# Reordering ScalarE's SSD distances and VectorE's decayed x in a one-core diffusion-backbone step

## What is computed

```
a_cs   = cumsum(dt * a)                                      # one row of 128 per head
lmat   = exp(a_cs[l] - a_cs[s]) where s is not later than l, else 0
y_diag = sum_s (C[l].B[s]) * lmat[l,s] * dt[s] * x[s]
states = sum_s B[s] * exp(a_cs[last] - a_cs[s]) * dt[s] * x[s]
y_off  = C[l] . states_in * exp(a_cs[l])
y      = (y_diag + y_off, both directions, + x * d_skip) * silu(z)
y      = rmsnorm over the 512 channels of the group
```

## Time and profile before

| What | Value |
|---|---|
| Median of three runs | 1797.37 us (1796.99 to 1802.09) |
| The profiled execution's own time | 1797.12 us |
| Its span (first to last recorded work) | 1795.3 us |
| TensorE busy | 1560.0 us (87%) |
| VectorE, ScalarE, GpSimd busy | 479.0, 324.8, 88.8 us |
| Mean granted TensorE clock | 0.976 of full |
| Units of the SSD stage | about 136 to 412 us of the span |

### The profile page before, as it was taken

One profiled execution on the slowest core, in us unless ns is written; L12 is line 12 of the kernel. 1 busy time (PEld: TensorE's weight loads), 2 busy tenths in 40 slices (PEclk: granted clock), 3 DMA queues, 4 the chain that ended last, 5 costly groups with the idle time before them and its releaser, 6 DMA issues.

```text
span 1795.3 us, 22496 instructions
## 1 busy us (share of the span) xinstructions
PE 1560.0 (87%) x9269; PEld 925.9 (52%) x9269; DVE 479.0 (27%) x1189; ACT 324.8 (18%) x893; POOL 88.8 (5%) x116
## 2 busy tenths in 40 slices
PE   6997988999999999998999888777878777977776
PEld 4654445455545555555666545444455444544443
DVE  2336666761003555524211110000010000100003
ACT  1336445440001222111110100000000000000001
POOL 0002122110000000100000000000000000000000
PEclk9998999999999999998999999999989999999999
DMA  8234333312431433465799999999999999999995
GB/s 342 94 108 164 106 106 124 134 59 94 187 117 59 188 141 123 168 261 200 318 428 426 429 427 427 427 427 429 426 417 427 427 427 428 427 427 427 428 427 227
DMA packets 40449, 512.91 MB, mean 286 GB/s; under 512 B 4624, under 2 KB 4752, under 8 KB 10528
## 3 DMA queue, kind: packets, MB, share of 16 engines
q1 hardware_dynamic: 34272, 489.89, 65.9%
q0 software_dynamic: 5936, 21.01, 3.5%
q10 hardware_dynamic: 144, 0.59, 0.1%
HBM read 506.65 MB, written 4.82 MB: 285 GB/s over the span
## 4 chain that ended last, share of the span: by engine, by line
PE 52%; DMA 31%; DVE 8%; ACT 6%; issue 2%; SPq 0%; DVEq 0%; ACTq 0%; POOL 0%
DMA arena<-in_expert_chunks 31%; PE psum L975 17%; PE psum L651 7%; PE psum L407 5%; PE psum L623 5%; PE psum L418 4%; ACT arena L1265 3%; PE psum L815 2%; PE psum L707 2%; PE psum L430 1%; ACT arena L1277 1%; PE psum L699 1%; PE psum L458 1%; DVE arena L1668 1%; PE psum L923 1%
## 5 line engine op out<-in xcount | busy, mean ns | idle before, releaser
L975 PE MATMUL psum<-arena 128*64 128x256 f32 x6144 | 708.7, 386 | 138.0 <-DMA arena<-in_expert_chunks 105.4
L975 PEld LDWEIGHTS psum<-arena 128*64 128x64 f32 x6144 | 442.0, 138 | 398.1 <-DMA arena<-in_expert_chunks 149.5
L2075 DVE TENSOR_TENSOR arena<-arena,psum 128x256 f32<-128x256 f32 x64 | 26.9, 421 | 704.8 <-ACT arena L1426 704.8
L407 PE MATMUL psum<-arena 128*128 128x384 f32 x512 | 168.9, 487 | 2.8 <-ACT arena L1184 2.8
L407 PEld LDWEIGHTS psum<-arena 128*128 128x128 f32 x512 | 96.2, 190 | 68.6 <-issue 3.3
L651 PE MATMUL psum<-arena 128*128 128x384 f32 x384 | 129.4, 491 | 0.0
L418 PE MATMUL psum<-arena 128*128 128x512 f32 x288 | 128.0, 600 | 0.0
L1426 ACT ACTIVATE arena<-psum 128x256 f32<-128x256 f32 x64 | 24.6, 384 | 563.4 <-PE psum L975 563.4
L1434 ACT ACTIVATE arena<-psum 32x256 f32<-32x256 f32 x126 | 47.3, 375 | 276.4 <-PE psum L975 275.3
L651 PEld LDWEIGHTS psum<-arena 128*128 128x128 f32 x384 | 72.5, 193 | 46.9 <-issue 3.0
L418 PEld LDWEIGHTS psum<-arena 128*128 128x128 f32 x288 | 55.8, 195 | 69.3 <-issue 68.5
(11 more groups left out here) (273 smaller groups left out, 1137.1 us busy)
## 6 DMA issues: line engine op xcount, KB each, us to landing
arena<-in_expert_chunks SPq DMA_DIRECT2D x191, 2048.0 KB, 25.4
arena<-in_mixer_chunks SPq DMA_DIRECT2D x40, 2048.0 KB, 8.3
arena<-cs_rows POOLq DMA_DIRECT2D x24, 512.0 KB, 4.9
arena<-in_h_cm POOLq DMA_DIRECT2D x8, 256.0 KB, 3.1
out_state<-arena POOLq DMA_DIRECT2D x8, 256.0 KB, 2.5
arena<-in_x_cm SPq DMA_DIRECT2D x1, 1536.0 KB, 8.6
arena<-in_expert_chunks SPq DMA_DIRECT2D x1, 1536.0 KB, 31.7
arena<-in_x_sample POOLq DMA_DIRECT2D x1, 1024.0 KB, 6.7
```

The source lines that it names most:

```text
L407: mm = pe.matmul(b[:, 0:NTOK], w[:, k, ct * P:(ct + 1) * P], src[:, k, :], start=k == 0, stop=k == KT - 1)
L975: mm = pe.matmul(psum[HALF * q:HALF * (q + 1), bank, 0:2 * P], src[:, k0 + k, :], w_k[:, 2 * P * q:2 * P * (q + 1)], start=bool(opens and ...
```

## The change

ScalarE makes `distances(1)` before the loop, and in unit u it makes `distances(u+2)` between the side items and the wait for `y_ready`, where it made `distances(u+1)` ahead of `decays(u+1)`. VectorE makes the chunk-0 `decayed` of both directions right after the three copies of x, and the other two behind the state copies of the same unit t = 0, so that t = 1 has none (and loses its wait for `x_ready`); `mean_square(u-1)` now comes behind `farther(u+1)` and ahead of `masked(u+1)`. No instruction is added or taken away.

```diff
             items([("z", 0, 2)])
+            distances(1)
             for u, (g, t) in enumerate(units):
                 if u + 1 < len(units):
-                    distances(u + 1)
                     decays(u + 1)
                 items(beside(g, t))
+                if u + 2 < len(units):
+                    distances(u + 2)
                 act.wait_ge(sem("y_ready"), u + 1)
@@
             for u, (g, t) in enumerate(units):
                 hd = slice(S_HPG * g, S_HPG * (g + 1))
-                if u:
-                    mean_square(u - 1)
                 if t == 0:
                     for tt in range(NT):
                         b = x_take()
                         x_free(dve.tensor_copy(xTM[:, tt, :], b[:, :]))
                     x_settle()
+                    decayed(0, 0, g)
+                    decayed(1, 0, g)
                 if u + 1 < len(units):
                     farther(u + 1)
+                if u:
+                    mean_square(u - 1)
+                if u + 1 < len(units):
                     masked(u + 1)
-                if t < 2:
-                    if t == 1:
-                        dve.wait_ge(sem("x_ready"), n_x[0])
-                    decayed(0, t, g)
-                    decayed(1, 2 * t, g)
                 if u:
                     rstd_of(u - 1)
@@
                         x_free(dve.tensor_copy(st_out[:, d, :], b[:, :]))
+                    decayed(0, 1, g)
+                    decayed(1, 2, g)
                 if t == 1:
```

## The result

The changed kernel takes 1769.86 us, the median of four runs (1766.51 to 1772.40), beside 1799.73 us for the kernel before in the runs it was compared with (four, 1796.99 to 1804.40). The ratio is 0.983 with a 95% interval of 0.9816 to 0.9844, some 30 us faster; the forecast was 1765 us. The profiled execution takes 1766.51 us with a span of 1764.7, 30.6 us less than the 1795.3 of before.

A forecast was written before the change was run, and what follows sets the result against it. The ScalarE-VectorE loop of square, distances and farther bounds the SSD stage, TensorE following. Gains 7.5 (group 0) + 21.6 (groups 1, 2) + 3.8 (group 3) = 32.9 us off 1797.12: 1764.2, given as 1765 us; eight in ten 1759 to 1777.

The forecast's parts named there:

- Rival B: Behind the SSD stage: the microseconds saved do not reach the end, total within 5 us of before; chance 0.03.
- t = 0, group 0: First unit of the stage: no square before it, so it only loses 1.2 us for the two decayed behind the state copies.
- t = 1, group 0: ScalarE's gap there is 2.68 us, so the distances come 2.1 us late and 3.3 us is gained.
- t = 2, group 0: Farther starts at y ready, with square, distances and handover no longer ahead of it: gain 5.4 us.
- t = 0, groups 1 and 2: Farther starts 2.3 us sooner, two decayed behind the state copies cost 1.2 us: net gain 1.1 us each.
- t = 1, groups 1 and 2: Farther starts at most 1.1 us late, as the distances overfill ScalarE's 3.71 us gap: gain 4.3 us each.
- t = 2, groups 1 and 2: Farther starts at y ready itself, the square beside it and the mean behind: gain 5.4 us each.
- group 3: TensorE binds there; its first state matmul starts at 4.0 us after y ready, not waiting for decayed x: gain 3.8 us.
- C: ScalarE stands at the late distances in all units, the farther waits 5.4 us as before: about 1801 us; chance 0.01.
- D: ScalarE's distances wait for their cumulative sums, rows landing over 15 us later, holding up the square: 1846 us; chance 0.02.
- rival A: TensorE takes over in groups 0 to 2, with 1.2 GHz spells after waits: gain 21 us, 1776 us; chance 0.13.
- loss bound: VectorE's two decayed at the t = 0 product's start: one decayed lost, 0.6 us a group, 2.4 us over four groups.

The follow-up runs named there:

- e1: Kernel before with only ScalarE's part of the change (distances made earlier), VectorE's order as before: 1770.41 us, ratio 0.9841 to the kernel before.
- e2: Changed kernel with ScalarE's loop of before, so only VectorE's part of the change: 1800.65 us, ratio 1.001 to the kernel before.
- e4: Changed kernel with distances of u+2 made before the first tanh in t = 0 and t = 1 of groups 0 to 2: 1762.75 us.
- e5: Changed kernel with both the second two decayed moved ahead of the weights and the distances made before the first tanh: 1758.68 us, ratio 0.9777.
- e6: Changed kernel with GpSimd's product cut to one head of eight, the other heads' weights in the chunk left at zero: 1753.52 us, ratio 0.9744.
- e7: Changed kernel with the mean of the square put back ahead of the copies and the farther: 1772.31 us, ratio 0.9851 to the kernel before.
- e3: Changed kernel with the second two decayed moved from behind the state copies to ahead of the weights of t = 0: 1764.54 us, ratio 0.9808.

## Why the prediction was right

**What bounds.** Right, and shown by e1 and e2: with the loop shortened the time goes although a part of TensorE's waits stays; with the waits for the decayed x removed and the loop left, they come back elsewhere and the time stays.

**That nothing is lost behind the stage.** Right. The span from L623's first matmul on is 1383.6 us before and 1383.2 after, and between 1382.0 and 1385.0 in all ten traces. Rival B falls.

**The sum.** Predicted 32.9 us for the profiled execution, 30.6 came. The stage itself gave 31.6; 1.5 us went ahead of it, where the change does nothing (below). Unit by unit:

| Term | predicted gain | measured |
|---|---|---|
| t = 0, group 0 | -1.2 | -1.0 |
| t = 1, group 0 | 3.3 | 4.1 |
| t = 2, group 0 | 5.4 | 4.5 |
| t = 0, groups 1 and 2 | 1.1 each | 1.7, 1.3 |
| t = 1, groups 1 and 2 | 4.3 each | 4.4, 4.4 |
| t = 2, groups 1 and 2 | 5.4 each | 4.5, 4.5 |
| group 3 | 3.8 | 3.3 |

That the sum came so near is in part luck. In group 0, 7.6 us for 7.5, two errors cancel: t = 2 gave 0.9 less and t = 1 gave 0.8 more. Unit 1 of the kernel before was 0.7 us longer than unit 4, because ScalarE stood 1.44 us at 183.16 for the z tile behind TensorE's wait of 7.76 us, where unit 4 has 0.52; in the changed kernel neither wait is there. The prediction, which let TensorE follow everywhere, had no term for it. The t = 0 units gave more than 1.1 us; between their own 1.7 and 1.3 stands the instruction held up by GpSimd's product, 3.08 us before in unit 3 and 2.72 in unit 6, 2.7 after in both.

**The distances' room.** Predicted 1.0 to 1.1 us late, 1.03 measured, and e4 got back 1.1, 1.1 and 2.1 us. Rivals C and D fall: in groups 1 and 2 no farther but those of t = 1 waits for the distances, and the distances at 245.98 us follow the tanh at 245.44 with no wait for their rows.

**The terms that were mis-sized.** First t = 2, 4.5 us instead of 5.4. The step counted VectorE and ScalarE and let TensorE follow. But TensorE waits 2.5 to 5.1 us at L605 in t = 1 and comes out of it with the clock granted in part at its 1.2 GHz level (0.50 of full over the four L605 matmuls in unit 1, 0.77 in unit 4), and the tile behind takes 8.18 us. So the second z tile is late: ScalarE stands 1.20 us for it in unit 5 and 2.19 in unit 2. This is rival A, come true in small, 0.9 us a group and not 4. That two so different delays cost the same has a reason in the rows: with either, VectorE's first L1561 comes beside GpSimd's product and ends 0.5 us behind it (262.54 us after a product that ends at 261.99 in unit 5; 200.33 after 199.79 in unit 2), and the second tanh and the second L1561 still follow. In e4, where the wait at L605 was 1.61 us, the slow tile was absent, the first of the two ran ahead of the product, and unit 5 took 16.14 us, the 16.3 that was predicted. In e5 it is unit 2 that takes 16.13 us, with a tile of 7.03 us behind a wait of 2.09, and unit 5 that takes 17.18, with a tile of 8.02 us behind one of 2.14. In e6, where the product is small, lateness costs its size: unit 2 stands 0.48 us for its z tile and takes 15.38 us, unit 5 does not and takes 14.8. No run changed this meeting by itself in the full kernel, so this part is read from the rows and not tried.

Second, group 3: TensorE arrived at the state matmuls 4.6 us after y was ready and not 4.0, since it was behind its own work and no longer waiting for the last bank of y. The wait that was foreseen there did not come for the same reason. And "what counts is when its first state matmul starts" holds only with the loop shortened: from there to the end of the stage it is 44.8 us before and 44.7 after, but 50.3 in e2.

Third, a slip that did no harm: a mean clock of 0.93 between full and half speed means that 0.14 of the time was at half speed, and the loss is 0.07 x 72.6 = 5 us; the prediction's words have the 0.07 as the time at half speed, its 5 us and its 56.5 are right, and e6 measured 56.8.

**VectorE beside GpSimd.** The product still meets one instruction, now L1547 at 2.71 us instead of L1546 at 3.08. The two decayed beside its start took 1.28 us together, as alone, so the loss bound that the rule of the Trainium skill ("SBUF — State Buffer", "Who interferes with whom") gave did not come. The rows do not speak against the rule itself: the product's row starts at 219.73, 0.3 us ahead of the end of the second decayed, and is 2.55 us long instead of 2.36, as if it had waited for it, and the next instruction with two SBUF inputs took the block. Which of two comes first can't be read to some tenths of a us, though: in the earlier trace rows L1546 starts 0.28 us ahead of the product and is the one held up. That the block is the product's doing is shown by e6, where it is gone with the product's size. What the product costs the changed kernel is at least the 5.4 us a group that e6 takes off (62.2 to 56.8 us), since TensorE binds from there on.

**The net of VectorE's edits.** The prediction gave the t = 0 decayed a gain and the open pair a loss, but costed the mean at nothing because it comes behind. That is right for its new place; e7 shows what the old one would have cost once the distances are out, 5.6 us. The gain of 2.3 us that it gave t = 0 came from the distances alone; beside e1, where both pairs are hidden behind ScalarE's copies, the first pair's new place nets nothing and the second's is a loss that e3 gets back.

## What to carry to other kernels

The list of waits names who came last, not what the time is for: here it named the decayed x, whose move alone gave nothing, while the chain of waits named an engine-to-engine loop that TensorE only followed. When work is taken out of such a loop, look for its new place, idle time long enough for it in every unit (here 3.7 us for 4.7 in one of three), and for what then waits first. Lateness does not simply add: 1.2 and 2.2 us of it cost the same 0.9 us here, because, by the rows, either pushed an instruction beside GpSimd's product. A trial with one half of a change each is the cheapest way to see which half works, and it takes both: ScalarE's half alone also removed more than half of the waits.

## What the runs showed that was not expected

The same code ahead of the stage takes 41.5 us in some executions and 44.3 in others. TensorE's timelines of before and after:

```profile
38.70 41.52 PE L407 MATMUL psum<-arena 128*128 128x384 f32 x128 [2.80 <-ACT arena L1184]
```

```profile
38.99 44.31 PE L407 MATMUL psum<-arena 128*128 128x384 f32 x128 [2.80 <-ACT arena L1184]
```

Both follow the same idle time of 2.80 us; the granted clock over the tile is 1.00 in the first and 0.94 in the second. Of the ten traces four have 41.5, five some 44.4 and one 43.0, whichever the kernel, so this is 3 us of scatter, in executions where the clock stands at its lower level for longer behind an idle spell. Behind a second one, of 2.41 us ahead of L516, the way to the stage takes 53.9 to 56.5 us, at a granted clock of 1.00 in the changed kernel, 0.93 in the one before and 0.89 in e4. Together the stage begins between 135.4 and 140.0 us, and a single execution can mislead by that much; the stage's own length, read between two of its matmuls, repeated to 0.1 us in the two traces of the changed kernel. The same shows at L605, and there the length of the wait alone does not decide: behind waits of 1.21, 1.61 and 2.09 us the four L605 matmuls took 1.98 to 1.99 us, behind 1.50 us in e6 they took 3.55, behind 2.14 us in e5 2.73 and the tile after them 8.02 instead of 7.03. What sets this apart was not tried and stays open.
